# One DMA from HBM to 128 partitions in place of a one-row load and a GpSimd broadcast

## The reference

```python
# es: the token's 128 experts, gs: their gates
a = jnp.einsum('td,ted->te', xs, u[es])              # one dot per token and picked expert
hact = jax.nn.gelu(a) * gs
out = jnp.einsum('te,ted->td', hact, v[es])
```

## Time and profile before

| | us |
|---|---|
| median of three runs | 4141.27 |
| lowest and highest of them | 4135.5, 4142.84 |
| the profiled execution, its own time | 4142.91 |
| its span, first to last instruction | 4141.2 |
| TensorE busy in the span | 3612.4 |
| VectorE busy | 2328.4 |
| GpSimd busy | 2207.0 |
| ScalarE busy | 1061.3 |

### The profile page before, as it was taken

How to read it: one execution, slowest core, us unless ns; L and a number is a source line. 1 busy time by engine, 2 the same in 40 slices (tenths; PEclk the granted TensorE clock), 3 DMA queues, 4 the chain that set the end, 5 groups by cost and what they waited for, 6 DMA issues and landing times.

```text
span 4141.2 us, 56272 instructions
## 1 busy us (share of the span) xinstructions
PE 3612.4 (87%) x17958; PEld 3033.3 (73%) x17958; DVE 2328.4 (56%) x3749; ACT 1061.3 (26%) x1464; POOL 2207.0 (53%) x1880
## 2 busy tenths in 40 slices
PE   6999977569879467588898898998999999999998
PEld 5788755457767456477887787887887888888886
DVE  2000015771158996577887787776555555555554
ACT  3122124432222123122222222222222222222221
POOL 3344434443355596776676666666454545444541
PEclk9999987789999788799999999999999999999999
DMA  3233310003322134566766766767777777777774
GB/s 121 76 91 96 87 38 1 0 20 122 101 73 80 41 152 176 181 218 220 235 228 218 234 226 216 235 225 229 232 237 227 237 238 235 232 230 237 237 231 143
DMA packets 320015, 689.11 MB, mean 166 GB/s; under 512 B 132784, under 2 KB 133040, under 8 KB 316976
## 3 DMA queue, kind: packets, MB, share of 16 engines
q1 hardware_dynamic: 233776, 417.51, 32.0%
q0 software_dynamic: 86160, 270.60, 19.6%
HBM read 656.53 MB, written 31.46 MB: 166 GB/s over the span
## 4 chain that ended last, share of the span: by engine, by line
PE 30%; DMA 11%; POOL 9%; issue 7%; DVE 2%; POOLq 1%; DVEq 0%; ACT 0%; ACTq 0%
DMA exp_u_rows<-in_u_rows,exp_now 9%; POOL exp_x_wide L1747 5%; PE exp_o L1815 5%; PE exp_o L1817 5%; PE exp_o L1819 5%; PE exp_a L1799 4%; PE exp_a L1803 4%; PE exp_a L1801 4%; PE exp_y L1847 3%; POOL exp_u_rows L1739 2%; DMA exp_x_row<-plain_rows_table 1%; POOL exp_x_row L1731 1%; DVE exp_u_rows L1914 1%; POOL exp_v_rows L1767 1%; DMA exp_v_rows<-in_v,exp_now 1%
## 5 line engine op out<-in xcount | busy, mean ns | idle before, releaser
L1815 PE MATMUL exp_o<-exp_vh,exp_ah 128*128 128x512 f32 x1536 | 633.0, 412 | 181.8 <-DVE h L1960 114.2
L1799 PE MATMUL exp_a<-x_high,exp_uh 128*128 128x384 f32 x2048 | 689.3, 337 | 8.1 <-DVE exp_ul L1904 8.1
L1803 PE MATMUL exp_a<-x_high,exp_ul 128*128 128x384 f32 x2048 | 685.8, 335 | 0.0
L1801 PE MATMUL exp_a<-x_low,exp_uh 128*128 128x384 f32 x2048 | 685.8, 335 | 0.0
L1767 POOL DMA_INDIRECT exp_v_rows<-in_v,exp_now x512 | 562.1, 1098 | 224.4 <-issue 120.7
L1817 PE MATMUL exp_o<-exp_vl,exp_ah 128*128 128x512 f32 x1536 | 618.2, 402 | 0.0
L1819 PE MATMUL exp_o<-exp_vh,exp_al 128*128 128x512 f32 x1536 | 615.8, 401 | 0.0
L1960 DVE TENSOR_TENSOR h<-h,exp_o 128x512 f32<-128x512 f32 x768 | 514.3, 682 | 158.9 <-PE exp_o L1819 158.9
L1815 PEld LDWEIGHTS exp_o<-exp_vh,exp_ah 128*128 128x128 f32 x1536 | 301.0, 196 | 299.8 <-DVE h L1960 133.9
L1866 ACT CAST exp_vh<-exp_raw 128x1024 fp32r<-128x1024 f32 x256 | 255.8, 1047 | 918.3 <-PE exp_o L1819 915.0
L1914 DVE SCALAR_TENSOR_TENSOR exp_u_rows<-exp_u_rows,exp_x_wide 128x1024 f32<-128x1024 f32 x256 | 330.1, 1290 | 267.3 <-DMA exp_u_rows<-in_u_rows,exp_now 231.1
(11 more groups left out here) (304 smaller groups left out, 5656.5 us busy)
## 6 DMA issues: line engine op xcount, KB each, us to landing
exp_raw<-in_u SPq DMA_DIRECT2D x256, 512.0 KB, 5.3
exp_raw<-in_v SPq DMA_DIRECT2D x256, 512.0 KB, 4.2
w_in_raw<-in_w_in SPq DMA_DIRECT2D x88, 512.0 KB, 3.6
gate_table<-table_stage SPq DMA_DIRECT2D x6, 4096.0 KB, 11.2
exp_gates<-gate_table SPq DMA_DIRECT2D x128, 192.0 KB
w_out_raw<-in_w_out SPq DMA_DIRECT2D x32, 512.0 KB, 3.7
w_q_raw<-in_w_q SPq DMA_DIRECT2D x32, 512.0 KB, 3.9
exp_v_rows<-in_v,exp_now POOLq DMA_INDIRECT x512, 4.1
```

Of the source, the lines that this page charges most:

```text
L1799: pe.matmul(bank, uh[:, b, c, :], xh[:, 0:DENSE_TB, c, :], start=(c == 0), stop=False)
L1801: pe.matmul(bank, uh[:, b, c, :], xl[:, 0:DENSE_TB, c, :], start=False, stop=False)
L1803: last = pe.matmul(bank, ul[:, b, c, :], xh[:, 0:DENSE_TB, c, :], start=False, stop=(c == DC - 1))
L1815: pe.matmul(o_bank[dc][:, :], ah[:, parity, b, tokens], vh[:, b, cols], start=(b == 0), stop=False)
```

## The change

The one-row buffer `x_row` and its semaphores go. Where GpSimd loaded a row to one partition and broadcast it, it now issues one DMA whose source is the row in HBM, read once for each of the 128 partitions (512 KB written). The function keeps the name `widen`. The order on GpSimd becomes take(0), widen(0), take(1), widen(1), take(2), widen(2), take(3), widen(3). `widen` has no wait of its own: it stands behind the `take` of the same q, whose wait for `dot_done` covers the half of `x_wide` that it writes. The dot waits for the DMA's semaphore.

```diff
-        x_row = [place(f"exp_x_row{s}", [1, HALF_D], F32, kb) for s, kb in enumerate((24, 28))]
...
-                def load_x(q):
-                    wait(pool, x_ready, a * QUADRANTS + (q - 1))
-                    pool.sem_inc(waited, 1)
-                    pool.dma_start(x_row[q % 2][0:1, :],
-                                   sparse["rows"][pl(row + q * ROWS_OF_QUADRANT, 1),
-                                                  half * HALF_D:(half + 1) * HALF_D])\
-                        .then_inc(x_row_in[q % 2], 16)
-
...
                 def widen(q):
-                    pool.wait_ge(x_row_in[q % 2], a * (8 * QUADRANTS) + 16 * (q // 2 + 1))
-                    pool.sem_inc(waited, 1)
-                    pool.partition_broadcast(x_wide[:, q % 2, :], x_row[q % 2][0:1, :])\
-                        .then_inc(x_ready, 1)
-
-                load_x(0)
-                load_x(1)
-                take(0)
-                take(1)
-                widen(0)
-                load_x(2)
-                widen(1)
-                load_x(3)
-                for q in (2, 3):
+                    pool.dma_start(x_wide[:, q % 2, :],
+                                   sparse["rows"][pl(row + q * ROWS_OF_QUADRANT, 1),
+                                                  half * HALF_D:(half + 1) * HALF_D]
+                                   .to_broadcast([P, HALF_D]))\
+                        .then_inc(x_wide_in[q % 2], 16)
+
+                for q in range(QUADRANTS):
                     take(q)
                     widen(q)
...
-                n = a * dots_of_group + q
                 dve.wait_ge(u_rows_in[q % 2], a * (8 * QUADRANTS) + 16 * (q // 2 + 1))
-                dve.wait_ge(x_ready, n + 1)
+                dve.wait_ge(x_wide_in[q % 2], a * (8 * QUADRANTS) + 16 * (q // 2 + 1))
```

More of the change, by code:

```diff
@@ L1632, in experts @@
         o_done, o_out, stored = sem("o_done"), sem("o_out"), sem("stored")
-        now_ready, x_ready, waited = sem("now_ready"), sem("x_ready"), sem("waited")
-        x_row_in = [sem(f"x_row_in{s}") for s in range(2)]
+        now_ready, waited = sem("now_ready"), sem("waited")
+        x_wide_in = [sem(f"x_wide_in{s}") for s in range(2)]
         rest_back = sem("rest_back")
@@ L1645, in experts @@
         units = DENSE_TB * (D // PC)
-        dots_of_group = QUADRANTS
         def wait(eng, s, value):
```

## The result

The changed kernel takes 4256.6 us (median of four runs, 4250.5 to 4263.7), the kernel before 4140.7. The ratio is 1.028, with a 95% interval of 1.026 to 1.030: 116 us slower, where 42 us faster was forecast. 4256.6 lies above 4225, the upper end of the range.

The account below looks back on a forecast made before the run. The bound was taken to be the dots stretch's loop of dot done, GpSimd free, gather, landing, next dot. 28 pairs, each 1.5 us shorter, give 42 us: 4142.9 - 42 = 4101, forecast 4100 us; range 4040 to 4225.

Parts of the forecast that it names:

- What bounds the kernel now: Last block's dots stretch: a dot-to-gather-to-dot loop, four turns of 9.8 us a pair of phases; at most 162 us to win.
- What is removed: On GpSimd: 256 broadcasts and 256 one-row loads, 491 us of its time; the gather then starts 0.83 us after its dot.
- The size of the landing: x DMA, issue to landing: 4.2 us low, 5.3 middle, 7.55 high; taken as 5.3, and 6.3 in the full stretch.
- u3: Fourth dot of a pair's u phase: forecast 1.5 us earlier than 2181.33 and still what is late next.
- The prediction's own sign of being wrong: In the profile after: x_wide landing at 6.5 us or more, or late raw u or v tiles holding the splits back.
- rival (B): Dots stretch: DMA engines become the bound; landing of 7.0 us gives 42.8 us a pair, 4245; middle 4190; chance 0.30.
- The step list: One pair's third and fourth u dots and first two v dots, timed step by step: 1.5 us earlier, times 28 pairs.
- (A): Dots stretch: landing under load cancels the gain, at a landing of 6.1 +- 0.1 us; 4142 us; chance 0.13.
- (C): Dots stretch: the stalls vanish at a landing of 4.2 us, most of 162 us come back; about 4000 us; chance 0.07.
- (D): x DMA: one-row source read by few engines or one after another, twice the landing; +500 us; chance 0.03.
- The DMA engines as a bound by their share rate: Dots stretch: 326 GB/s at a share of one makes 13.0 MB take 39.9 us a pair, +22 us, 4164.
- The slower dots beside the broadcasts: VectorE's dots: mean 1290 ns against median 1226, up to 16 us of VectorE time; not counted, left in the range.

Follow-up runs that it names:

- experiment 9: Changed kernel with four halves of u_rows and x_wide, gather and x DMA of dot n waiting for dot n-3: 3985.2 us, ratio 0.962 to the kernel before.
- experiment 1: Changed kernel with the x DMA writing one partition only (4 KB), the other 127 zero: 4052.9 us, ratio 0.980 to the kernel before.
- experiment 4: Changed kernel with four halves of x_wide, x DMA of dot n+2 issued behind the gather of dot n: 4086.9 us, ratio 0.988 to the kernel before.
- experiment 2: Changed kernel with 128 different table rows as source of the x DMA, same bytes: 4245.0 us, ratio 1.026 to the kernel before.
- experiment 5: Kernel before with the same 512 KB x DMA added behind each gather, into a spare buffer no dot waits for: 4289.9 us, ratio 1.035.
- experiments 6 and 7: Changed kernel with 256 KB of x: first to 64 partitions only, 4244.1 us; then half of each row to all 128 partitions, 4130.2 us.
- experiment 3: Changed kernel with the two DMAs of a dot swapped, x first and then the gather: 4301.6 us, ratio 1.040 to the kernel before.
- experiment 8: Changed kernel with four halves of u_rows and x_wide, gather and x DMA of dot n waiting for dot n-4: 4041.0 us, ratio 0.976.

## Why the prediction was wrong

- **What bounds the kernel now**: right. The stretch is a loop of "dot done, GpSimd free, gather, landing", and 162 us was a fair ceiling: experiment 9 gets 155 us.
- **What is removed**: right in mechanism and larger than counted. In the 224 steady dots the gather starts 0.82 us after its dot in the median and 1.09 us at most (forecast 0.83), and the removal is worth about 88 us (experiment 1).
- **The size of the landing**: the term of the sum that was wrong. 5.3 us, and 6.3 for u3, was taken; 7.2 was measured over all dots. By place in the 28 pairs the medians are 6.6 us for u2, 8.0 for u3, 8.5 for v0, 5.2 for v1, and 8.7 for u1. The prediction's own sign of being wrong, a landing of 6.5 us or more, was met. The working itself had the deciding point, L = 6.1 us, and the price: at L = 7.0 a pair takes 42.8 us. Measured, 224 dots from 1784.7 us (the end of the 32nd dot) to 2983.1 are 28 pairs of 42.8 us. So the number is that of rival (B), with a chance of 0.30, at its stated value of 4245 us and not at the 4190 that I put in its middle. That it fits so closely is partly luck: the same formula gives 43.6 us a pair at the measured 7.2, and VectorE hardly waits at all before u2, v0 and v1. And the name of (B), the DMA engines as the bound, isn't what the runs show: the same bytes pass 170 us faster in experiment 4. The 32 first dots add some 10 us, as the working said for its middle landing (+9), where I counted nothing.
- **Two slips in the sums**, too small to change anything: the 0.2 us between landing and dot is missing at u3, so the smallest shift is 1.3 us and the sum 37 us in place of 42; and 5.5 less 1.2 is 4.3 us, not 4.2.
- **Why 5.3 was the wrong row**: it is the landing of one transfer at a share of 0.69. Here the x DMA goes out 1 us behind a 512 KB gather of the same queue, so it lands behind it (1.9 us behind, in the median), and the change itself raises the load, to 0.86. The place and the load were both written down, and then the transfer was priced by the row of the old load. How much of the 7.2 us is the place in the queue and how much the load stays open.
- **The step list was too short.** It followed u2, u3, v0 and v1, where the kernel before stood still, and stopped. u1 had no idle time in the pair read, so it was not worked out; but its gather had landed only 0.2 us before the dot, 6.1 of the 6.3 us from its issue (2162.90) were used up. It has the largest new wait: 124 us more idle time of VectorE over the 28 pairs, and 6.63 us in the pair shown, where it holds the splits and with them TensorE's v phase. u3, which was worked out, has 89 us more where 1.5 us a pair less was forecast.
- **(A) and (C)**: (C), at about 4000 us, did not come from this change, but experiment 9 shows that the idle time can be had. **(D)** is refuted by experiment 2. **The DMA engines as a bound by their share rate** (39.9 us a pair) is refuted too: experiment 9 moves 380 GB/s.
- **The slower dots beside the broadcasts**: the dot's mean went from 1290 to 1223 ns, 17 us of VectorE time in 256 dots, as counted. What this gave in the kernel's time was not measured.

The account of the 116 us, by experiments 1 and 4: removing GpSimd's work gains about 88 us (4141 to 4053); 134 MB of traffic beside the loop cost about 34 (4053 to 4087, experiment 1 against 4); waiting for that traffic inside the loop costs 170 (4087 to 4257). The middle step compares two kernels that differ in the place of x as well as in its bytes, so its 34 us are the least sure of the three. Beside the old loop the same traffic cost up to 149 us (experiment 5), so it has no one price that carries from one loop to the other.

## What to carry to other kernels

When an on-chip copy becomes a DMA, look first at where the dot waits for it: a second large transfer inside a two-buffer loop costs its landing at the new load, behind the first one in its queue, in every turn that has no slack. The same transfer issued one turn earlier was a gain here. Work out every step of the loop that has no slack, also those at which nothing waits yet, and price a transfer by the load that the change makes. And more buffers have a best depth: letting transfers out for three dots ahead beat four, with the raw v tiles of the other queue landing in 9.0 us in place of 16.1.

## What the runs showed of the hardware

- One core alone moved 380 GB/s over 810 us at a share of 1.03, while TensorE was busy 98% of the time (experiment 9). The Trainium skill, page "DMA: Bandwidth & Descriptors", section "Specifications", puts a core's HBM limit at about 358 GB/s, half of a stack that two cores share; this run of a kernel on one core stands above it.
- A DMA from GpSimd to 64 partitions (256 KB) took almost as long as one to 128 (512 KB): 6.6 and 7.2 us to landing (experiments 6 and 7).
- The issue of a gather on GpSimd rose from 968 to 1516 ns (median) when it stood right behind another DMA's issue (experiment 3). Why is open.
- 128 reads of one 4 KB row in HBM, against reads of 128 rows, made 11.6 us of difference in 256 transfers, with overlapping intervals (experiment 2).
- The same 512 KB load of the SP queue landed in 4.0, 6.7, 9.0 or 16.1 us (medians of raw v in 1790 to 2600 us), at 225 GB/s before, 302 after, 380 in experiment 9 and 356 in experiment 8. So the landing doesn't follow the rate alone.
